# GpSimd takes over the differential pairs' combination in a two-block transformer kernel

## The chip, the cores and the metric

The kernel runs on one core of one Trainium2 chip. Its time is the device time of one execution in microseconds (us), and a kernel's number is the median of several executions. The core has a matrix engine (TensorE, PE in the rows; PEld is its weight load), a vector engine (VectorE, DVE), a scalar engine (ScalarE, ACT), GpSimd (POOL) and SyncE (SP), which starts most transfers. They run side by side and wait for each other by semaphores. Each works off its own list strictly in order.

## What is computed

Two transformer blocks of two layers each run one after the other over 512 tokens of width 1024, in float32 ("three-product" matmuls split each operand in a high and a low part). The change touches only the attention of the second block. It has three kinds of heads:

```python
# second block, hybrid_layer: 6 "a" heads (dilated), 4 "b" heads (differential), 6 "c" heads (causal)
def probs(q, k):                     # one 128-row block of queries
    s = jnp.einsum('bqhd,bkhd->bhqk', sl(q), k).astype(jnp.float32) * scale + bias
    return jax.nn.softmax(jnp.where(causal, s, -jnp.inf), axis=-1)
a = probs(q1, k1) - lam * probs(q2, k2)
return jnp.einsum('bhqk,bkhd->bqhd', a.astype(v.dtype), v)
...
o_b = (rms_norm(o_b, subln_g, SUBLN_EPS) * (1.0 - lam_init)).astype(x.dtype)
...
heads = jnp.concatenate([o_a.reshape(Bn, S, -1), o_b.reshape(Bn, S, -1), o_c.reshape(Bn, S, -1)], axis=-1)
h = layer_norm(DEEPNORM_ALPHA * x + heads @ w_o, ln1_g, ln1_b)
```

A differential head thus needs two score matrices, whose exponentials are combined as first + ratio * second (the ratio has the sign, lambda and both row sums in it) before they meet the values.

## The kernel before

The attention of a layer is a list of 80 units (`UNITS`): one head and one block of 128 queries each, 128, 256, 384 or 512 keys wide (the block's row i gives 128(i+1) keys). A "b" head takes two units that stand next to each other, `first` and `second`; there are 16 such pairs. The first 8 units (`EARLY`, four pairs) are worked off among the projections. The other 12 pairs, whose `second` is unit 9, 13, 18, 23, 28, 33, 38, 42, 47, 52, 57 or 62, are spread among 48 units of "a" and "c" heads. For this loop every engine has its own list by steps. In step s:

- TensorE makes the scores of unit s (`score`, lines 2248, 2249 and 2252) into one of three PSUM banks, then the transposes of unit s-4 (line 2367; a pair only has those of its `second`, which wait for the combination, `s_paired`). Two ranks after a group's last transposes `mix` multiplies the group's transposed probabilities with the values (line 2346). After a head's last group `turn_chunk` transposes a 128-column chunk of the output `ao` (line 2325), in the steps of `turn_at`.
- VectorE adds mask and bias and takes the row minimum or maximum (`scored`, line 2986), from PSUM into one of five SBUF buffers `sc2` ("sc" in the rows). A buffer is taken again five units later, when its unit was transposed, or, for a `first`, when its pair was combined. Then come, if due, `pair(s-2)` (two small operations for the ratio, lines 2994 and 2995, and one SCALAR_TENSOR_TENSOR over the unit, line 2996), `rows_out2` (divides a finished group's rows by their sums into `ao`, lines 3050 to 3062), and `lo_part` (the low part of a transposed chunk, `g_lo`, line 2530). `sub_norm` (lines 3025 to 3033) normalises the "b" heads' output.
- ScalarE takes the exponentials (`exp2`) and copies the transposes out of PSUM. At steps 24 and 26 it also splits a weight tile.
- GpSimd makes the copies of the keys (`two_keys`, lines 944 and 947, four operations for each "a" head), each when the scores of a named unit are there, and low parts of weight tiles (line 927).

So a pair goes TensorE, VectorE, ScalarE, VectorE, TensorE. A semaphore between two engines, or between two dependent operations of one engine, stands at each arrow.

Of the kernel before, what the change touches and what calls it, by code (L numbers as in the profile page):

```python
# [262 lines left out]
def _program(nc, I, out, seen):  # L263
    ctx = ExitStack()
    with ctx:
# [211 lines left out]
        s_pool_piece = Signal(nc, ctx, seen, "pool_piece")  # L477
        s_product = Signal(nc, ctx, seen, "product")
        s_b_recip = Signal(nc, ctx, seen, "b_recip")
        s_rows_part = Signal(nc, ctx, seen, "rows_part")  # L480
# [289 lines left out]
        ended = {what: GROUPS[group_of[r]][-1] for what, r in last_of.items()}  # L770
        out_step = {what: turn_step[r + 3] if r + 3 <= LAST else STEPS for what, r in ended.items()}
        B_DONE = max(out_step["b", h] for h in range(B_HEADS))
# [143 lines left out]
        def _(pool):  # L916
# [14 lines left out]
            def ctx_lo(l, k):  # L931
# [3 lines left out]
                                   ALU.subtract).then_inc(s_lo_c.sem, s_lo_c.nth((l, k)))  # L935

            def two_keys(y, h):

# [52 lines left out]
            for i, what in enumerate(splits):  # L991
# [19 lines left out]
                if what[1:] == ("o", 0, 0):  # L1011
# [8 lines left out]
                    pool.wait_ge(s_mm.sem, s_mm.at((what[0], "vc", XT - 1)))  # L1020
                    pool.memset(vc[:].rearrange("p t (h d) -> p (t h) d", d=VW)[:, :, HD:VW], 1.0).then_inc(s_vc_ones.sem, s_vc_ones.nth(what[0]))
                if what[1:] == ("o", 0, 1):
                    pool.wait_ge(s_tile_lo.sem, s_tile_lo.at(splits[i - 1]))
                    for h in range(A_HEADS):
                        two_keys(what[0], h)
                for p in range(-(-width(what) // PIECE)):
# [667 lines left out]
        def _(pe):  # L1694
# [475 lines left out]
            for l in range(DEPTH):  # L2170
# [181 lines left out]
                for step in range(FROM, STEPS):  # L2352
# [3 lines left out]
                    if r is not None:  # L2356
# [3 lines left out]
                        if UNITS[i]["second"]:  # L2360
                            pe.wait_ge(s_paired.sem, s_paired.at((y, i)))
                        else:
                            pe.wait_ge(s_probs.sem, s_probs.at((y, i)))
# [151 lines left out]
        def _(dve):  # L2515
# [422 lines left out]
            for l in range(DEPTH):  # L2938
# [50 lines left out]
                def pair(i):  # L2989

                    u = UNITS[i]
                    n, ratio = u["n"], small[:, 2, i % 8:i % 8 + 1]
                    dve.wait_ge(s_probs.sem, s_probs.at((y, i)))
                    step(V.reciprocal(ratio, small[:, 1, i % 8:i % 8 + 1]))
                    step(V.tensor_scalar(ratio, ratio, sums[:, u["sum"]:u["sum"] + 1], lam[:, 4:5], ALU.mult, ALU.mult))
                    V.scalar_tensor_tensor(probs_of(i)[:, 0:n], probs_of(i)[:, 0:n], ratio, probs_of(i - 1)[:, 0:n],
                                           ALU.mult, ALU.add).then_inc(s_paired.sem, s_paired.nth((y, i)))
# [68 lines left out]
                for st in range(EARLY, STEPS):  # L3066
                    if st - 2 == EARLY + 1:
                        pair(st - 2)
                    if turns(st) is not None and turns(st) >= 3:
                        rows_out2(turns(st) - 3)  # L3070
                    if st < len(UNITS):
                        u = UNITS[st]
                        if st >= EARLY + N_B and UNITS[st - N_B]["first"]:
                            dve.wait_ge(s_paired.sem, s_paired.at((y, st - N_B + 1)))
                        elif st >= EARLY + N_B:
# [8 lines left out]
                    sub_norm(st)  # L3084
                    if st - 2 in turn_at:
                        k = turn_at[st - 2]
                        dve.wait_ge(s_kr_all.sem, s_kr_all.at((y, C_HEADS - 1)))
                        lo_part(g_lo[:, CHUNKS.index(k), :], ps[:, TURNED["chunk", k], :], g_hi[:, CHUNKS.index(k), :], (y, "m", k), (y, "m", k))
                assert B_DONE + 2 < STEPS
                for r in range(LAST - 2, LAST + 1):  # L3090
                    rows_out2(r)
# [235 lines left out]
```

## Time and profile before

| | us |
|---|---|
| median of 3 runs | 1830.54 (1830.51 to 1833.87) |
| the profiled execution | 1828.74 |
| its span in the profile | 1826.9 |
| attention loop, first layer of the second block | 744.4 to 823.6 |
| attention loop, second layer | 1342.3 to 1421.5 |

Busy over the span: PE 1779.0 us (97%), DVE 1196.8 (66%), ACT 912.8 (50%), POOL 777.8 (43%). TensorE's granted clock is 0.998 of full speed. The profiled execution lasts 1.84 us longer than its span. Times of events are counted from the span's start. Each of the two loops runs from the scores of unit 10 to the end of the last `mix`.

### The profile page before, as it was taken

Reading aid. Unit: us, or ns where it says so; the run is one execution under the profiler, and the core shown is the slowest. Engines: PE = TensorE matmul, PEld = TensorE weight load, DVE = VectorE, ACT = ScalarE, POOL = GpSimd, SP = SyncE. Lnnn points to the kernel's source line nnn. Section 1 sums busy time; section 2 is a strip of 40 time slices with the busy share of each in tenths; the row PEclk is TensorE's granted clock in tenths of the full one; section 3 lists DMA queues with packets and bytes.
Section 4 is the critical chain, followed back from the end, with each engine's and each line's share of the span. In section 5 each row is a group of like instructions: output and inputs, shape, how many; then the busy total and the mean of one; then the engine's idle time right before and its main releaser. Section 6 shows DMA issues by size and latency. Waiting matters only on the chain.

```text
span 1826.9 us, 33474 instructions
## 1 busy us (share of the span) xinstructions
PE 1779.0 (97%) x13078; PEld 1585.0 (87%) x13078; DVE 1196.8 (66%) x2313; ACT 912.8 (50%) x1789; POOL 777.8 (43%) x601
## 2 busy tenths in 40 slices
PE   9999999999999999989999999999998999999997
PEld 7898888878898888678999998888877899999886
DVE  5797465269455353785999984256368589998533
ACT  4242276484366474883545443227488255444323
POOL 2544262255553454344443436544424354343652
PEclk9999999999999999999999999999999999999999
DMA  8444141123221232103232323222310323323321
GB/s 337 168 173 167 24 116 60 69 70 139 104 48 55 88 102 107 42 2 139 93 111 98 116 93 126 100 88 92 117 42 2 138 72 114 116 93 116 116 93 46
DMA packets 37032, 182.40 MB, mean 100 GB/s; under 512 B 8288, under 2 KB 9184, under 8 KB 18956
## 3 DMA queue, kind: packets, MB, share of 16 engines
q1 hardware_dynamic: 30664, 168.89, 26.5%
q10 hardware_dynamic: 6212, 11.36, 2.0%
q8 instruction: 106, 1.74, 0.4%
q14 instruction: 50, 0.41, 0.1%
HBM read 178.10 MB, written 5.41 MB: 100 GB/s over the span
## 4 chain that ended last, share of the span: by engine, by line
PE 85%; DVE 8%; ACT 4%; issue 2%; POOL 1%; DMA 1%; DVEq 0%; SPq 0%; ACTq 0%
PE ps L1718 17%; PE ps L1720 17%; PE ps L1719 17%; PE ps L2441 7%; PE ps L2443 7%; PE ps L2442 7%; PE ps L1798 2%; PE ps L1812 2%; PE ps L2346 2%; PE ps L2252 2%; PE ps L1779 1%; PE ps L2367 1%; DVE sc L2986 1%; POOL w_lo L927 1%; ACT pt L1184 1%
## 5 line engine op out<-in xcount | busy, mean ns | idle before, releaser
L927 POOL TENSOR_TENSOR w_lo<-raw,w_hi 128x512 fp32r<-128x512 f32 (+1 forms) x343 | 477.9, 1426 | 616.1 <-ACT w_hi L1057 615.9
L1057 ACT ACTIVATE w_hi<-raw 128x1024 fp32r<-128x1024 f32 (+3 forms) x174 | 170.9, 1026 | 225.8 <-PE ps L1720 208.8
L1033 POOL TENSOR_TENSOR w_lo<-raw,w_hi 128x512 fp32r<-128x512 f32 x80 | 112.7, 1408 | 222.9 <-ACT w_hi L1122 222.7
L1718 PE MATMUL ps<-h_hi,w_lo 128*128 128x512 f32 (+1 forms) x496 | 177.2, 357 | 3.7 <-DVE h_lo L2530 3.6
L1719 PE MATMUL ps<-h_lo,w_hi 128*128 128x512 f32 (+1 forms) x496 | 174.5, 352 | 0.0
L1720 PE MATMUL ps<-h_hi,w_hi 128*128 128x512 f32 (+1 forms) x496 | 174.5, 352 | 0.0
L1718 PE MATMUL ps<-w_hi,hid_lo 128*128 128x512 f32 x352 | 137.1, 390 | 0.0
L1719 PE MATMUL ps<-w_lo,hid_hi 128*128 128x512 f32 x352 | 137.0, 389 | 0.0
L1720 PE MATMUL ps<-w_hi,hid_hi 128*128 128x512 f32 x352 | 136.9, 389 | 0.0
L2530 DVE TENSOR_TENSOR hid_lo<-hid,hid_hi 128x512 fp32r<-128x512 f32 x44 | 65.4, 1529 | 102.1 <-ACT hid_hi L1158 102.1
L1718 PE MATMUL ps<-w_hi,g_lo 128*128 128x512 f32 (+3 forms) x320 | 114.1, 356 | 1.5 <-POOL w_lo L927 1.5
L1720 PE MATMUL ps<-w_hi,g_hi 128*128 128x512 f32 (+3 forms) x320 | 112.1, 350 | 0.0
L1719 PE MATMUL ps<-w_lo,g_hi 128*128 128x512 f32 (+3 forms) x320 | 111.8, 349 | 0.0
L1718 PEld LDWEIGHTS ps<-h_hi,w_lo 128*128 128x128 f32 x496 | 93.8, 189 | 18.6 <-issue 5.5
L1720 PEld LDWEIGHTS ps<-h_hi,w_hi 128*128 128x128 f32 x496 | 93.7, 189 | 12.9
L1719 PEld LDWEIGHTS ps<-h_lo,w_hi 128*128 128x128 f32 x496 | 93.8, 189 | 11.7
L2592 DVE SCALAR_TENSOR_TENSOR acc<-raw,cond,acc 128x512 f32<-128x512 f32 x112 | 98.9, 953 | 0.8 <-DMA raw<-in_tiles 0.7
L1122 ACT ACTIVATE ext_hi<-ps 128x512 fp32r<-128x512 f32 x80 | 47.8, 598 | 95.1 <-DVE ps L3163 69.6
L2441 PE MATMUL ps<-T_hi,w_lo 128*128 128x256 f32 x320 | 90.7, 283 | 0.0
L2441 PE MATMUL ps<-G_hi,w_lo 128*128 128x256 f32 x320 | 90.6, 283 | 0.0
L2442 PE MATMUL ps<-G_lo,w_hi 128*128 128x256 f32 x320 | 90.6, 283 | 0.0
L2443 PE MATMUL ps<-G_hi,w_hi 128*128 128x256 f32 x320 | 90.6, 283 | 0.0
(392 smaller groups left out, 5446.0 us busy)
## 6 DMA issues: line engine op xcount, KB each, us to landing
raw<-in_tiles SPq DMA_DIRECT2D x139, 1024.0 KB, 4.8
strips<-bias_rows ACTq DMA_DIRECT2D x18, 256.0 KB, 4.0
raw<-in_tiles SPq DMA_DIRECT2D x4, 832.0 KB, 4.2
bias_rows<-bias_row SPq DMA_DIRECT2D x10, 320.0 KB, 9.9
raw<-in_tiles SPq DMA_DIRECT2D x4, 768.0 KB, 5.1
res<-in_x SPq DMA_DIRECT2D x2, 1024.0 KB, 6.4
ln<-in_ln_g ACTq DMA_DIRECT2D x4, 512.0 KB, 5.0
ln<-in_ln_b ACTq DMA_DIRECT2D x4, 512.0 KB, 7.6
```

The costliest lines, as they stand in the source:

```text
L927: pool.tensor_tensor(w_lo[:, i % SPLIT, a:e], raw_of(what)[:, a:e], w_hi[:, i % SPLIT, a:e].bitcast(F32), ALU.subtract).then_inc(s_tile_lo ...
L1033: pool.tensor_tensor(lo, quad_of(what[0], j, name), hi.bitcast(F32), ALU.subtract).then_inc(s_pool_piece.sem, s_pool_piece.nth(((what[0], ...
L1057: act.activation(w_hi[:, i % SPLIT, a:b], raw_of(what)[:, a:b], ACT.Copy).then_inc(s_tile_hi.sem, s_tile_hi.nth((what, n)))
L1122: act.activation(piece_of(y, j, name)[0], src, ACT.Copy).then_inc(s_piece_hi.sem, s_piece_hi.nth((what, name)))
L1718: pe.matmul(o, lhs[1], rhs[0], start=first, stop=False)
L1719: pe.matmul(o, lhs[0], rhs[1], start=False, stop=False)
L1720: return pe.matmul(o, lhs[0], rhs[0], start=False, stop=last)
L2441: pe.matmul(o, lhs[1], rhs[0], start=starts and k == 0, stop=False, skip_group_check=True)
L2442: pe.matmul(o, lhs[0], rhs[1], start=False, stop=False, skip_group_check=True)
L2443: m = pe.matmul(o, lhs[0], rhs[0], start=False, stop=ends and k == 3, skip_group_check=True)
L2530: V.tensor_tensor(dst, src, hi.bitcast(F32), ALU.subtract).then_inc(s_lo.sem, s_lo.nth(key))
L2592: V.scalar_tensor_tensor(to[:], w, by, to[:], ALU.mult, ALU.add).then_inc(s_weigh.sem, s_weigh.nth((what, k, h)))
```

## The change

VectorE still computes the ratio of the 12 late pairs. The SCALAR_TENSOR_TENSOR over the unit leaves its list and becomes two operations of GpSimd: a multiplication by the ratio in place (TENSOR_SCALAR), a wait for itself, and the addition of the first's probabilities (TENSOR_TENSOR). TensorE, and VectorE before it reuses the first's buffer, wait for GpSimd. GpSimd's copies of the keys are put among these pairs. Besides, `rows_out2` comes one rank later in VectorE's list, the chunks' transposes (`turn_at`) and `sub_norm` one step later as a result, and `lo_part` one more step behind the transposes. The four early pairs stay as they were.

```diff
-        out_step = {what: turn_step[r + 3] if r + 3 <= LAST else STEPS for what, r in ended.items()}
+        out_step = {what: turn_step[r + 4] if r + 4 <= LAST else STEPS for what, r in ended.items()}
...
+            SECONDS = [x for x in range(EARLY, len(UNITS)) if UNITS[x]["second"]]
+            SOON_PAIRS = [x for x in SECONDS if x < 26]
+            LATE_PAIRS = [x for x in SECONDS if x >= 26]
+
+            def keys_behind(h):
+
+                scored = SCORED_LAST["c", 3 + h] if h < 3 else SCORED_LAST["a", h - 3]
+                return max(x for x in LATE_PAIRS if x <= max(scored, LATE_PAIRS[0]))
+
+            def pool_pair(y, x):
+
+                n = UNITS[x]["n"]
+                pool.wait_ge(s_ratio.sem, s_ratio.at((y, x)))
+                p_ = probs_of(x)[:, 0:n]
+                pool.tensor_scalar(p_, p_, small[:, 2, x % 8:x % 8 + 1], None, ALU.mult).then_inc(s_weighted.sem, s_weighted.nth((y, x)))
+                pool.wait_ge(s_weighted.sem, s_weighted.at((y, x)))
+                pool.tensor_tensor(p_, p_, probs_of(x - 1)[:, 0:n], ALU.add).then_inc(s_pool_paired.sem, s_pool_paired.nth((y, x)))
+                pool.wait_ge(s_pool_paired.sem, s_pool_paired.at((y, x)))
...
+                    for x in SOON_PAIRS:
+                        pool_pair(what[0], x)
                 if what[1:] == ("o", 0, 1):
                     pool.wait_ge(s_tile_lo.sem, s_tile_lo.at(splits[i - 1]))
-                    for h in range(A_HEADS):
-                        two_keys(what[0], h)
+                    for x in LATE_PAIRS:
+                        pool_pair(what[0], x)
+                        for h in range(A_HEADS):
+                            if keys_behind(h) == x:
+                                two_keys(what[0], h)
...
-                            pe.wait_ge(s_paired.sem, s_paired.at((y, i)))
+                            if i > EARLY:
+                                pe.wait_ge(s_pool_paired.sem, s_pool_paired.at((y, i)))
+                            else:
+                                pe.wait_ge(s_paired.sem, s_paired.at((y, i)))
...
-                    step(V.tensor_scalar(ratio, ratio, sums[:, u["sum"]:u["sum"] + 1], lam[:, 4:5], ALU.mult, ALU.mult))
+                    m = V.tensor_scalar(ratio, ratio, sums[:, u["sum"]:u["sum"] + 1], lam[:, 4:5], ALU.mult, ALU.mult)
+                    if i > EARLY:
+                        m.then_inc(s_ratio.sem, s_ratio.nth((y, i)))
+                    else:
+                        step(m)
+                    if i > EARLY:
+                        return
                     V.scalar_tensor_tensor(probs_of(i)[:, 0:n], probs_of(i)[:, 0:n], ratio, probs_of(i - 1)[:, 0:n],
                                            ALU.mult, ALU.add).then_inc(s_paired.sem, s_paired.nth((y, i)))
...
-                    if turns(st) is not None and turns(st) >= 3:
-                        rows_out2(turns(st) - 3)
+                    if turns(st) is not None and turns(st) >= 4:
+                        rows_out2(turns(st) - 4)
...
-                            dve.wait_ge(s_paired.sem, s_paired.at((y, st - N_B + 1)))
+                            dve.wait_ge(s_pool_paired.sem, s_pool_paired.at((y, st - N_B + 1)))
...
-                    if st - 2 in turn_at:
-                        k = turn_at[st - 2]
+                    if st - 3 in turn_at:
+                        k = turn_at[st - 3]
                         dve.wait_ge(s_kr_all.sem, s_kr_all.at((y, C_HEADS - 1)))
                         lo_part(g_lo[:, CHUNKS.index(k), :], ps[:, TURNED["chunk", k], :], g_hi[:, CHUNKS.index(k), :], (y, "m", k), (y, "m", k))
+                for k in [turn_at[s] for s in sorted(turn_at) if s + 3 >= STEPS]:
+                    lo_part(g_lo[:, CHUNKS.index(k), :], ps[:, TURNED["chunk", k], :], g_hi[:, CHUNKS.index(k), :], (y, "m", k), (y, "m", k))
...
-                for r in range(LAST - 2, LAST + 1):
+                for r in range(LAST - 3, LAST + 1):
```

GpSimd's list in the first layer's loop, before, from the keys of the third "a" head to those of the fourth (free_hi and free_lo hold a head's keys in high and low part):

```order
L944 CAST free_hi_155<-ka 64x512 [waits scores,k_low]
L944 CAST free_hi_155<-ka 64x512 [waits k_twice]
L947 TENSOR_TENSOR free_lo_158<-ka,free_hi_155 64x512 [waits k_twice]
L947 TENSOR_TENSOR free_lo_158<-ka,free_hi_155 64x512 [waits k_low]
L944 CAST free_hi_153<-ka 64x512 [waits scores,k_low]
L944 CAST free_hi_153<-ka 64x512 [waits k_twice]
L947 TENSOR_TENSOR free_lo_156<-ka,free_hi_153 64x512 [waits k_twice]
L947 TENSOR_TENSOR free_lo_156<-ka,free_hi_153 64x512 [waits k_low]
```

The same stretch of the changed kernel:

```order
L966 CAST free_hi_155<-ka 64x512 [waits scores,pool_paired]
L966 CAST free_hi_155<-ka 64x512 [waits k_twice]
L969 TENSOR_TENSOR free_lo_158<-ka,free_hi_155 64x512 [waits k_twice]
L969 TENSOR_TENSOR free_lo_158<-ka,free_hi_155 64x512 [waits k_low]
L954 TENSOR_SCALAR sc_4_149<-sc_4_149,small 128x128 [waits ratio,k_low]
L956 TENSOR_TENSOR sc_4_149<-sc_4_149,sc_3_148 128x128 [waits weighted]
L966 CAST free_hi_153<-ka 64x512 [waits scores,pool_paired]
L966 CAST free_hi_153<-ka 64x512 [waits k_twice]
L969 TENSOR_TENSOR free_lo_156<-ka,free_hi_153 64x512 [waits k_twice]
L969 TENSOR_TENSOR free_lo_156<-ka,free_hi_153 64x512 [waits k_low]
L954 TENSOR_SCALAR sc_4_149<-sc_4_149,small 128x384 [waits ratio,k_low]
L956 TENSOR_TENSOR sc_4_149<-sc_4_149,sc_3_148 128x384 [waits weighted]
```

The pairs of units 52 (128 wide) and 57 (384 wide) now stand behind four key operations each, which wait for scores of their own.

VectorE's list before, from the finished rows of a group ahead of unit 63 to the combination of pair 62 (ISA is `scored`, with a second row for its row result):

```order
L3053 RECIPROCAL recips<-sums 128x1
L3056 RECIPROCAL recips<-ps 128x4 [waits mixed]
L3057 TENSOR_TENSOR ao<-ps,recips 128x4x64 [waits dve_step]
L3062 TENSOR_SCALAR ao<-ps,recips 128x64 [waits b_recip]
L2986 ISA sc_0_145,small<-ps,strips 128x256 [waits scores,strips,turned]
L2986 ISA small 128x1
L2986 ISA sc_1_146,small<-ps,strips 128x512 [waits scores,strips,turned]
L2986 ISA small 128x1
L2994 RECIPROCAL small<-small 128x1 [waits probs]
L2995 TENSOR_SCALAR small<-small,sums,lam 128x1 [waits dve_step]
L2996 SCALAR_TENSOR_TENSOR sc_4_149<-sc_4_149,small,sc_3_148 128x256 [waits dve_step]
```

The same place of the changed kernel:

```order
L3016 ISA sc_0_145,small<-ps,strips 128x256 [waits scores,strips,turned]
L3016 ISA small 128x1
L2560 TENSOR_TENSOR g_lo<-ps,g_hi 128x512 [waits hi,kr_all]
L3089 RECIPROCAL recips<-sums 128x1
L3092 RECIPROCAL recips<-ps 128x4 [waits mixed]
L3093 TENSOR_TENSOR ao<-ps,recips 128x4x64 [waits dve_step]
L3098 TENSOR_SCALAR ao<-ps,recips 128x64 [waits b_recip]
L3016 ISA sc_1_146,small<-ps,strips 128x512 [waits scores,strips,turned]
L3016 ISA small 128x1
L3024 RECIPROCAL small<-small 128x1 [waits probs]
L3025 TENSOR_SCALAR small<-small,sums,lam 128x1 [waits dve_step]
```

Unit 63's `scored` has moved ahead of the group's rows, a chunk's low part (which stood before unit 62) has come in between, and both now stand between `scored` of unit 63 and `scored` of unit 64, which the ratio follows. The combination itself is gone.

## Rows read from the trace of the kernel before

**Rows 1.** Busy time by stage, the attention loop of each layer; (x) counts instructions.

```profile
core 0: us, PE busy (x) PEld busy (x) DVE busy (x) ACT busy (x) POOL busy (x), PEclk, DMA share, GB/s
744.40:823.60 79.20, 69.98 (x942) 56.72 (x942) 60.65 (x236) 65.82 (x171) 30.84 (x34) 1.00 0.08 22
1342.30:1421.50 79.20, 69.97 (x942) 56.73 (x942) 60.63 (x236) 65.80 (x171) 30.82 (x34) 1.00 0.08 22
```

**Rows 2.** Waits of PE in the first layer's loop: total us, times, longest.

```profile
PE ps L2367 <- DVE sc L2996: 6.8, 8, 1.5
PE ps L2346 <- DVE g_lo L2530: 0.8, 1, 0.8
PE ps L2252 <- DVE small L2986: 0.8, 1, 0.8
```

**Rows 3.** DVE groups by form, same loop: busy us, mean ns, idle before.

```profile
L3057 DVE TENSOR_TENSOR ao<-ps,recips 128x256 f32<-128x256 f32 x12 | 5.1, 425 | 1.0 <-PE ps L2346 0.6
...
L2530 DVE TENSOR_TENSOR g_lo<-ps,g_hi 128x512 fp32r<-128x512 f32 x5 | 3.5, 692 | 3.6 <-ACT g_hi L1616 3.6
...
L2996 DVE SCALAR_TENSOR_TENSOR sc<-sc,small,sc 128x512 f32<-128x512 f32 x3 | 3.1, 1036 | 0.1
...
L2996 DVE SCALAR_TENSOR_TENSOR sc<-sc,small,sc 128x256 f32<-128x256 f32 x3 | 2.4, 795 | 0.1
...
L2996 DVE SCALAR_TENSOR_TENSOR sc<-sc,small,sc 128x128 f32<-128x128 f32 x3 | 2.0, 661 | 0.1
...
L3056 DVE RECIPROCAL recips<-ps 128x4 f32<-128x4 f32 x11 | 1.9, 174 | 4.3 <-PE ps L2346 4.2
L2996 DVE SCALAR_TENSOR_TENSOR sc<-sc,small,sc 128x384 f32<-128x384 f32 x3 | 1.9, 619 | 0.1
```

**Rows 4.** The chain that ended last, 766.5 to 770 us; start us, us, what.

```profile
766.72 0.69 DVE sc L2986
...
767.84 0.76 DVE sc L2996
...
768.65 0.66 PE ps L2367 x4
```

**Rows 5.** POOL groups by form, whole span.

```profile
L947 POOL TENSOR_TENSOR free_lo<-ka,free_hi 64x512 fp32r<-64x512 f32 x24 | 31.5, 1314 | 1.9
L944 POOL CAST free_hi<-ka 64x512 fp32r<-64x512 f32 x24 | 14.6, 610 | 34.6 <-PE ps L2252 21.0 <-PE ps L2249 12.8
...
L969 POOL CAST q_parts<-q 64x768 fp32r<-64x768 f32 x6 | 4.9, 822 | 16.1 <-PE ps L1779 16.0
...
L927 POOL TENSOR_TENSOR w_lo<-raw,w_hi 128x128 fp32r<-128x128 f32 x4 | 2.9, 718 | 0.0
...
L927 POOL TENSOR_TENSOR w_lo<-raw,w_hi 128x16 fp32r<-128x16 f32 x1 | 0.2, 224 | 0.0
```

**Rows 6.** POOL in order of time; brackets hold idle before and releaser.

```profile
787.68 2.96 POOL L947 TENSOR_TENSOR free_lo<-ka,free_hi 64x512 fp32r<-64x512 f32 x2
792.87 1.28 POOL L944 CAST free_hi<-ka 64x512 fp32r<-64x512 f32 x2 [2.23 <-PE ps L2249]
794.24 2.65 POOL L947 TENSOR_TENSOR free_lo<-ka,free_hi 64x512 fp32r<-64x512 f32 x2
```

**Rows 7.** DVE in order of time, around two of the combinations.

```profile
787.90 1.61 DVE L2996 SCALAR_TENSOR_TENSOR sc<-sc,small,sc 128x512 f32<-128x512 f32 x1
...
797.33 0.62 DVE L2996 SCALAR_TENSOR_TENSOR sc<-sc,small,sc 128x384 f32<-128x384 f32 x1
```

**Rows 8.** PE in order of time: the first transposes of one combined unit.

```profile
798.01 0.55 PE L2367 MATMUL ps<-ident,sc 128*128 128x128 f32 x3 [0.66 <-DVE sc L2996]
```

**Rows 9.** DVE in order of time, the end of the loop.

```profile
809.72 1.22 DVE L3025 TENSOR_TENSOR sq_b<-ao 128x1024 f32<-128x1024 f32 x1
...
814.31 0.69 DVE L2530 TENSOR_TENSOR g_lo<-ps,g_hi 128x512 fp32r<-128x512 f32 x1
```

**Rows 10.** PE in order of time, the end of the loop.

```profile
815.05 1.39 PE L2346 MATMUL ps<-va,raw 128*64 128x65 f32 x40
```

More of the change, by code:

```diff
@@ L478, in _program @@
         s_product = Signal(nc, ctx, seen, "product")
+        s_ratio = Signal(nc, ctx, seen, "ratio")
+        s_pool_paired = Signal(nc, ctx, seen, "pool_paired")
+        s_weighted = Signal(nc, ctx, seen, "weighted")
         s_b_recip = Signal(nc, ctx, seen, "b_recip")
```

## The prediction

> **What bounds the kernel now.** The table of busy time comes first: TensorE is busy for 97% of the span, so a change elsewhere can only act where TensorE is not. I then cut the two attention loops of the second block out, the only stretches in which the changed lists differ. In each, 79.2 us long, TensorE is busy for 70.0 us, ScalarE 65.8, VectorE 60.6 and GpSimd 30.8 [rows 1]. The two layers agree to 0.02 us, so I work one out and double it. TensorE idles 9.2 us per layer; the list of who waited for whom says for what: 6.8 us, in 8 of the 12 late pairs, for the combined probabilities of line 2996; 0.8 for a low part, and 0.8 for a score bank that VectorE had not emptied [rows 2]. So all 12 combinations are on the path or near it, and eight have no slack at all.
>
> The next question is what is late in such a wait: VectorE's throughput or the length of the way round. At pair 28, the chain goes from TensorE's scores through `scored` (766.72, 0.69 us), the ratio, the combination (767.84 to 768.60) to the transposes at 768.65 [rows 4]. VectorE had idled before, and nothing but the length of the way counts. VectorE is itself the late one at two of the eight, pairs 47 and 62: there the combination is stretched, 1.61 us at 787.90 for a form whose mean is 1.04 and includes this one [rows 3, 7], and the longest wait of TensorE, 1.5 us, is for pair 62 [rows 2].
>
> **The change, part by part (per layer).**
>
> *The combination itself.* VectorE's twelve cost 3.1 + 1.9 + 2.4 + 2.0 = 9.4 us as measured, stretched ones included [rows 3]; with a start 0.02 us behind the ratio [rows 4] 9.6. GpSimd's first operation, a multiplication in place, is not in the trace. The nearest rows are casts, also with one input: 0.61 us for 512 columns, 0.82 for 768 [rows 5], so 0.19 + 0.00083 per column. Nothing in the trace says that a one-input operation can be faster than that cast, so it is the lower bound; the upper one is its two-input operation, 1.31 us for 512. I take the cast: 0.61, 0.50, 0.40, 0.29 us for 512, 384, 256, 128 columns. The second is the two-input form: 1.31 us for 512, 0.22 for 16 [rows 5], so by a straight line 1.02, 0.75, 0.47 for the others (the 128-column row says 0.72, which is my upper bound for that width). A start behind another operation takes 0.09 us (794.15 to 794.24) [rows 6]; there are two. That makes 2.10, 1.71, 1.33 and 0.94 us, three times each: 18.2 us. The way round gets 18.2 - 9.6 = 8.6 us longer over twelve pairs. Four pairs, two of 384 and two of 128 columns, are not waited for now; on the path they would be worth 2 x (1.71 - 0.64) + 2 x (0.94 - 0.68) = 2.7 us, and I count half. **Term a: 8.6 - 1.3 = 7.3 us.**
>
> *The shared list of GpSimd.* Four key operations take 4.0 us (792.87 to 796.89) [rows 6], and a pair behind them waits for all four. They were free to run late, since their "a" heads come steps later. Now the ratio of pair 47 is there at 787.90 [rows 7]: GpSimd is done with it at 790.0, with the third keys at 794.0, with pair 52 at 794.9, with the fourth keys at 798.9. The ratio of pair 57 is ready at 797.3 [rows 7], and TensorE stands waiting for that pair now (0.66 us at 798.01) [rows 8]. It starts 1.6 us late, less the 0.4 by which pair 47's own longer product moves both. **Term b: 1.2 us.** The keys themselves stay hidden.
>
> *VectorE's list.* Behind `scored` of unit 63 now stand a low part (0.69 us) and a group's rows (0.17 + 0.42 and two small ones, about 0.8 in sequence) [rows 3], then `scored` of unit 64 and the ratio of pair 62. Before, the low part was two places earlier and the rows ahead of unit 63. At worst 1.2 us of this comes out at TensorE, and 0.35 and 0.4 at pairs 23 and 28, where rows now stand in front of the last `scored` ahead of a ratio. Against it VectorE loses waits: 4.2 us for `mix` ahead of the rows and 3.6 for ScalarE ahead of the low parts [rows 3]. These helped nobody by being there, but most of them lie where the next `scored` waits for TensorE's scores anyway, so their end gives little. I take half. **Term c: 1.0 us.**
>
> *The end of the loop.* The chunk of step 73 (before 72) has its low part in step 76 (before 74). It frees the PSUM bank of the `mix` that TensorE has in step 77. Now it ends at 815.00 and `mix` starts at 815.05 [rows 9, 10]: no slack. In between come two more `scored` and a group's rows (0.4 + 0.7 + 0.6 us), of which VectorE has some in hand since it need not wait for `mix`. **Term d: 1.0 us.**
>
> *What costs nothing:* the new semaphores on TensorE (a wait replaces a wait), and VectorE's wait for GpSimd before it reuses a `first`'s buffer. Behind it are queued the `scored` four and five units after the pair's second. TensorE needs their banks only after the pair's own transposes, so its wait covers this one; without that cover it would cost up to the 1.3 us by which a 512-column product is longer. The early pairs, and all work outside the loops, do not change; no transfer moves.
>
> *A rule on the memory ports.* VectorE's combination took 1.61 us at 787.90 while GpSimd ran two-input operations from 787.68, which themselves took 2.96 us against 2.65 for the same two at 794.24 [rows 6, 7]; at 767.84, with GpSimd idle, 0.76 was enough [rows 4]. My sum contains this stretch as a gain, since it goes by the measured 9.4 us and leaves VectorE with almost nothing of this kind. What is left is the squaring at 809.72, 1.22 us, with two inputs from SBUF [rows 9]: the last keys, which move behind pair 62, could now run beside it. The Trainium skill (SBUF — State Buffer, "SBUF: two separate sides") says that GpSimd and a VectorE operation with two SBUF inputs take the shared port pair as an exclusive lock, held for the whole instruction. By that rule the squaring would wait for up to one GpSimd operation, 1.3 us by the row of such a one, and term d would be 2.2 instead of 1.0, the time 2.4 us longer in all. The rows of the combination bear the lock out; that the squaring meets it is open, and I leave it out.
>
> *Sum:* 7.3 + 1.2 + 1.0 + 1.0 = 10.5 us per layer, 21 in both. The profiled execution has 1828.7 us (its span, 1826.9, and 1.8 around it), so 1849.7. The median of the runs shown is 1.8 us above that execution: **1851.5 us.**
>
> **The rivals.**
>
> *Faster: VectorE's relief decides.* It loses 9.4 us of operations and up to 7.8 us of waits per layer [rows 3]. If VectorE were what is late at most pairs, the ratio would come earlier by as much as the product is longer. Pairs 47 and 62 speak for it, and the 0.8 us for a score bank [rows 2]; pair 28 and the idle before it speak against. It decides where the ratio comes more than 1.3 us earlier. With all 8.4 us of the three waits gone the time would be 1814; with the half of it that those places could give, 4 us per layer, 1822. Chance 0.11.
>
> *No change.* The relief and the longer way cancel: 1827 to 1834. Chance 0.07. That the move is not made is excluded: the lists show it.
>
> *Partly absorbed.* Lateness at one pair is taken up by slack before the next, as after unit 62, and the list terms vanish; half of term a or somewhat more stays: 3 to 7 us per layer, 1837 to 1844. For it speaks that TensorE does not wait at four pairs. Chance 0.24.
>
> *More costly.* If GpSimd's multiplication costs as much as its two-input operation, each product is 0.7, 0.5, 0.35 or 0.2 us longer, 5.2 us per layer, so 1862; with the squaring's 2.4 it is 1864. Chance 0.10.
>
> **How the numbers follow.** The forecast (8 to 14 us per layer: 1846 to 1859) has 0.48. Slower by more than 0.2%, about what a measurement of this kernel can tell from no change (3.7 us), are the forecast, the partly absorbed and the more costly case, 0.82; the same 0.07; faster 0.11. The range leaves out the faster case and the lowest of "no change", and above only what is beyond the sum of both upper bounds: 1832 to 1866. Slower cases alone would be 1837 to 1864.
>
> **What would show it.** In the changed profile each loop is about 10 us longer, with TensorE's busy time still near 70 us. TensorE's largest wait at the transposes is for GpSimd's addition, some 12 to 17 us per layer, in nine or more pairs. GpSimd's operations on "sc" number 24 per layer and sum to about 16 us; the multiplication of 512 columns takes about 0.6 us (above 1 would be the costly case). The longest wait is at pair 57, behind key copies. VectorE's busy time in the loop falls by about 9 us, and its waits for `mix` ahead of the rows nearly vanish. The last `mix` but two waits for a low part. I would be wrong if the ratios came much earlier after the pair's scores than now, in other words if the stretch from `scored` of a second's follower to its ratio shrank by over 1 us at most pairs, or if GpSimd's operations were much shorter than the rows of its casts.

## The result, and the profile after

The changed kernel takes 1888.2 us (median of 4, 1884.3 to 1891.6) against 1830.5 (1829.6 to 1833.9): ratio 1.031, 95% interval 1.029 to 1.033. It is slower by 57.7 us, where 21 were forecast, and lies outside the range of 1832 to 1866. The profiled execution has a span of 1882.5 us.

The two loops, cut so that each holds the same 942 matmul records as in [rows 1]:

```profile
core 0: us, PE busy (x) PEld busy (x) DVE busy (x) ACT busy (x) POOL busy (x), PEclk, DMA share, GB/s
745.40:851.60 106.20, 78.66 (x942) 62.79 (x942) 52.33 (x224) 66.92 (x171) 53.62 (x58) 0.90 0.06 16
1370.20:1477.00 106.80, 78.25 (x942) 63.20 (x942) 53.09 (x224) 66.89 (x171) 53.66 (x58) 0.92 0.06 16
```

They take 106.2 and 106.8 us instead of 79.2, together 54.6 of the 55.6 us by which the span grew. The last 1.0 us lies ahead of the loops; executions of the kernel before alone differ by more. TensorE's idle time rose from 9.2 to 27.5 us in the first, and its busy time from 70.0 to 78.7, for the same work: the granted clock, 1.00 before, is 0.90. VectorE is busy 8.3 us less, GpSimd 22.8 more.

What TensorE and VectorE wait for in the first layer's loop (us, times, longest):

```profile
PE ps L2397 <- POOL sc L956: 24.5, 11, 4.0
PE ps L2373 <- DVE g_lo L2560: 2.4, 2, 1.5
```

```profile
DVE sc L3016 <- POOL sc L956: 20.2, 10, 2.9
...
DVE recips L3092 <- PE ps L2373: 1.2, 1, 1.2
```

Where [rows 2] had 6.8 us in eight places for VectorE's combination, there are 24.5 in eleven for GpSimd's addition. The second list shows a wait that the prediction put at no cost: VectorE, now behind GpSimd for a `first`'s buffer, stands for 20.2 us (whether that costs time is taken up below). Its wait for `mix` ahead of the rows went from 4.2 us [rows 3] to 1.2, as forecast.

GpSimd's groups by form (busy us, mean ns), 3 of each kind per layer:

```profile
L954 POOL TENSOR_SCALAR sc<-sc,small 128x512 f32<-128x512 f32 x3 | 4.7, 1567 | 3.2 <-DVE small L3025 3.2
L956 POOL TENSOR_TENSOR sc<-sc,sc 128x512 f32<-128x512 f32 x3 | 3.8, 1263 | 0.3
L954 POOL TENSOR_SCALAR sc<-sc,small 128x384 f32<-128x384 f32 x3 | 3.7, 1245 | 4.5 <-DVE small L3025 4.4
...
L956 POOL TENSOR_TENSOR sc<-sc,sc 128x384 f32<-128x384 f32 x3 | 3.0, 992 | 0.2
L954 POOL TENSOR_SCALAR sc<-sc,small 128x256 f32<-128x256 f32 x3 | 2.8, 924 | 14.6 <-DVE small L3025 14.6
L956 POOL TENSOR_TENSOR sc<-sc,sc 128x256 f32<-128x256 f32 x3 | 2.2, 723 | 0.2
L954 POOL TENSOR_SCALAR sc<-sc,small 128x128 f32<-128x128 f32 x3 | 1.8, 605 | 12.9 <-DVE small L3025 12.8
L956 POOL TENSOR_TENSOR sc<-sc,sc 128x128 f32<-128x128 f32 x3 | 1.4, 454 | 0.2
```

The addition came out as worked out from [rows 5] (1.26, 0.99, 0.72, 0.45 us against 1.31, 1.02, 0.75, 0.47). The multiplication costs 1.57, 1.25, 0.92 and 0.61 us, where 0.61, 0.50, 0.40 and 0.29 were put and 1.31 for 512 columns was the upper bound. With the two starts of 0.09, twelve products make 25.5 us, not 18.2, against VectorE's 9.6.

Some of TensorE's waits in order of time (start us, us; in brackets the idle time before), and below them its granted clock by stretches of 5 us (the value ahead of the last two):

```profile
751.80 1.11 PE L2397 MATMUL ps<-ident,sc 128*128 128x128 f32 x4 [3.55 <-POOL sc L956]
...
771.05 0.44 PE L2397 MATMUL ps<-ident,sc 128*128 128x128 f32 x2 [2.00 <-POOL sc L956]
```

```profile
779.95 0.66 PE L2397 MATMUL ps<-ident,sc 128*128 128x128 f32 x4 [3.95 <-POOL sc L956]
```

```profile
750.00:755.00 5.00, 3.20 (x22) 2.12 (x24) 0.87 (x4) 0.33 (x2) 1.67 (x2) 0.50 0.02 3
755.00:760.00 5.00, 3.79 (x41) 2.75 (x38) 1.97 (x9) 3.02 (x8) 1.06 (x2) 0.83 0.25 63
765.00:770.00 5.00, 3.46 (x17) 2.10 (x17) 3.52 (x18) 3.48 (x9) 1.27 (x2) 1.00 0.03 8
775.00:780.00 5.00, 1.05 (x8) 0.69 (x6) 2.02 (x13) 2.26 (x7) 3.89 (x3) 1.00 0.00 0
780.00:785.00 5.00, 5.00 (x37) 3.95 (x39) 1.40 (x7) 3.13 (x9) 0.00 (x0) 0.66 0.01 3
```

After the wait of 3.55 us the clock of the stretch is 0.50 (1.2 instead of 2.4 GHz all the time), after that of 3.95 it is 0.66, while from 760 to 780, with waits of 1.21, 0.79 and 2.00 us, it is 1.00. A lower clock also follows the waits of 2.60, 3.42 and 3.01 us at pairs 42, 57 and 62. The profile before has no wait above 1.51 us in the loops and no such stretch. The four transposes at 751.80 take 1.11 us; four at 779.95, just before the clock falls, 0.66.

The first loop reads as if long waits made the clock fall and short ones did not. The second does not bear that out. There the clock falls behind the wait of 2.00 us at pair 23, and stays at 1.00 behind one of 3.47 us at pair 62:

```profile
1395.26 0.69 PE L2397 MATMUL ps<-ident,sc 128*128 128x128 f32 x2 [2.00 <-POOL sc L956]
...
1454.91 0.44 PE L2397 MATMUL ps<-ident,sc 128*128 128x128 f32 x2 [3.47 <-POOL sc L956]
```

```profile
1395.00:1400.00 5.00, 4.74 (x63) 4.13 (x64) 1.40 (x4) 2.79 (x6) 4.92 (x5) 0.66 0.01 2
...
1455.00:1460.00 5.00, 5.00 (x85) 4.70 (x85) 2.23 (x9) 3.46 (x9) 4.65 (x6) 1.00 0.01 3
```

### The profile page after: what moved, and what is told of

Same layout as the page of the kernel before. It is cut to its first block, busy times and chain, and to the rows that moved or that the text cites. A ratio compares the mean times of both kernels' runs of the same rounds, so it can differ in the third digit from the quotient of the medians.

```text
span 1882.5 us, 33520 instructions
## 1 busy us (share of the span) xinstructions
PE 1796.8 (95%) x13078; PEld 1598.5 (85%) x13078; DVE 1181.1 (63%) x2289; ACT 914.6 (49%) x1789; POOL 822.9 (44%) x649
## 4 chain that ended last, share of the span: by engine, by line
PE 83%; DVE 7%; POOL 4%; ACT 4%; issue 2%; DMA 1%; DVEq 0%; SPq 0%; POOLq 0%; ACTq 0%
PE ps L1745 17%; PE ps L1747 16%; PE ps L1746 16%; PE ps L2471 7%; PE ps L2473 7%; PE ps L2472 7%; PE ps L1825 2%; PE ps L1839 2%; PE ps L2397 2%; PE ps L2373 2%; PE ps L1806 1%; POOL sc L954 1%; PE ps L2279 1%; POOL sc L956 1%; ACT w_hi L1084 1%
## 5 line engine op out<-in xcount | busy, mean ns | idle before, releaser
L2397 PE MATMUL ps<-ident,sc 128*128 128x128 f32 x300 | 59.6, 304 | 49.5 <-POOL sc L956 49.5
L1747 PEld LDWEIGHTS ps<-h_hi,w_hi 128*128 128x128 f32 x496 | 93.7, 189 | 12.9
L2397 PEld LDWEIGHTS ps<-ident,sc 128*128 128x128 f32 x300 | 39.6, 154 | 66.1 <-POOL sc L956 54.8
```

The lines of the kernel that those rows point to most:

```text
L1747: return pe.matmul(o, lhs[0], rhs[0], start=False, stop=last)
L2397: m = pe.transpose(ps[:, b, P * j:P * j + P], probs_of(i)[:, P * j:P * j + P], ident[:])
```

## The experiments

Times are medians, and ratios are to runs of the kernel before made together with each kernel (its medians: 1830.0 to 1831.3 us). Excesses over it are against these.

**The list change alone.** The kernel before, VectorE combines:

```diff
-        out_step = {what: turn_step[r + 3] ...
+        out_step = {what: turn_step[r + 4] ...
...
-                        rows_out2(turns(st) - 3)
+                        rows_out2(turns(st) - 4)
...
-                    if st - 2 in turn_at:
+                    if st - 3 in turn_at:
...
```

> The kernel before with only the second half of the change: rows_out2 one rank later, the chunks' transposes one step later, lo_part three steps behind them; VectorE still combines. Theory A (GpSimd's longer product on TensorE's way round is the loss, the clock falls in its wake): this part alone costs little, 1827 to 1837 us (my terms c and d were 2 us per layer, of which VectorE's saved waits may give some back), TensorE's granted clock stays at full speed. Theory L (the later rows and low parts are what TensorE waits for): a third or more of the loss, 1848 us or more.

1844.2 us, ratio 1.006 (1.005 to 1.008), 12.9 us slower: between the two theories, and three times terms c and d. Of the 15.5 us by which its span is longer, 3.6 lie ahead of the loops, where nothing was changed; each loop is 5.9 us longer. TensorE's clock does fall (0.98 in both loops), which theory A had excluded.

**GpSimd's part alone,** the changed kernel with those lines set back:

> The changed kernel with the list part undone: GpSimd combines the twelve pairs, rows_out2, turn_at and lo_part stand as before. Theory A: nearly the whole loss stays, 1880 to 1895 us. Theory L: 1870 us or less.

1881.3 us, ratio 1.027 (1.026 to 1.029), as theory A said. GpSimd's part is 50 of the 57.7 us, and the lists add only 6.9 on top of it, where alone they cost 12.9: some of their lateness may hide behind the longer products (no run shows where).

**A cheaper multiplication.** First a copy in place (it leaves the ratio out of the result), then a multiplication in another form, each in place of the same line (arguments are left out at "..."):

```diff
-                pool.tensor_scalar(p_, p_, small[...], None, ALU.mult)...
+                pool.tensor_copy(p_, p_)...
```

```diff
-                pool.tensor_scalar(p_, p_, small[...], None, ALU.mult)...
+                pool.tensor_tensor(p_, p_, small[...].broadcast_to((P, n)), ALU.mult)...
```

> The changed kernel with GpSimd's multiplication by the ratio replaced by a plain copy in place (the ratio is left out of the result). The copy's rows of before say 0.61 us for 512 columns against 1.57 measured for the multiplication; over the twelve pairs the product gets shorter by 3 x (0.96 + 0.75 + 0.52 + 0.32) = 7.7 us per layer. Theory A: TensorE's waits fall by about that, 15 us in all, and most of the slow-clock stretches (9 us of longer matmuls per layer) go with the long waits: 1858 to 1874 us. Theory L or a loss by the mere number of hand-overs: the waits hardly depend on the product's length, 1883 us or more.

> The changed kernel, with GpSimd's multiplication written as a two-input operation that reads the ratio as a column repeated over the width; the result is the same. Theory L (the length of the product is what TensorE waits for, at all twelve pairs): the addition, also of two inputs, took 1.26, 0.99, 0.72 and 0.45 us for 512, 384, 256 and 128 columns, the multiplication 1.57, 1.25, 0.92 and 0.61, so each product is 0.31, 0.25, 0.20 or 0.15 us shorter, three times each: 2.7 us per layer, 5.5 us in all, and up to 2 more where TensorE's clock then does not fall: 1881 to 1884. Theory H (what counts is the number of hand-overs and the place in GpSimd's list, not the length): 1887 to 1889. A third case, that the repeated column is read as slowly as before: no change in the rows of line 954, 1887 to 1889.

The copy: 1870.1 us, ratio 1.021 (1.020 to 1.023). The two-input form: 1880.0 (1871.9 to 1881.8), ratio 1.027 (1.025 to 1.028); its profiled execution is the fastest one. In their profiles, first the copy's, then the other's:

```profile
L954 POOL COPY sc<-sc 128x512 f32<-128x512 f32 x3 | 1.8, 610 | 1.8 <-DVE small L3025 1.5 <-POOL free_lo L969 0.3
```

```profile
L954 POOL TENSOR_TENSOR sc<-sc,small 128x512 f32<-128x512 f32 x3 | 3.1, 1040 | 3.4 <-DVE small L3025 3.1 <-POOL free_lo L969 0.3
```

The copy costs what the prediction gave the multiplication (0.61 us). The multiplication of two inputs, the second a repeated column, costs 1.04 us, less than the addition and two thirds of the one-input form. Theory L's 1881 to 1884 rested on 1.26 us for it; it was shorter, 8.8 us in all instead of 5.5, and 8.2 us came back, with executions 10 us apart. All four lie below theory H's range, so theory L holds. The copy's time lies in theory A's range, but half of the reason given failed: the slow-clock stretches did not go with the shorter products. The clock is 0.91 and 0.90 in its loops, and TensorE is busy as long as in the changed kernel (table below).

**The addition alone** (the ratio is left out of the result):

> The changed kernel without GpSimd's multiplication: only the addition stands (this leaves the ratio out of the result). A product is then 1.26, 0.99, 0.72 or 0.45 us long, 11.4 us per layer with starts, where the copy in place made 17.9, the two-input multiplication 21.2 and the changed kernel 25.6. Theory L (time goes by the summed length of the products, with the clock's fall in it; the copy gave 18.1 us for 15.3 us of length, 1.18 per us): 13.0 us less length than with the copy, 13 to 15.4 us less time, 1855 to 1857. Theory F (a floor: other waits, the ratio's own way or the moved rows, take over): 1860 or more.

1851.3 us, ratio 1.011 (1.009 to 1.013), less than either theory said. The loops in the profiled executions (columns as in [rows 1]), of the addition alone, of the copy, and of the list change alone from above:

```profile
747.05:837.25 90.20, 75.23 (x942) 59.74 (x942) 52.20 (x224) 66.18 (x171) 40.68 (x46) 0.94 0.07 19
1355.90:1444.70 88.80, 73.82 (x943) 58.80 (x942) 52.22 (x224) 66.23 (x172) 40.71 (x46) 0.96 0.07 20
```

```profile
746.70:844.70 98.00, 77.92 (x941) 63.04 (x942) 52.10 (x224) 66.77 (x171) 46.05 (x58) 0.91 0.07 18
1363.30:1463.00 99.70, 79.21 (x943) 64.02 (x942) 52.33 (x225) 66.79 (x172) 46.15 (x58) 0.90 0.06 18
```

```profile
747.95:833.10 85.15, 72.40 (x942) 58.05 (x942) 58.85 (x236) 66.53 (x171) 30.86 (x34) 0.98 0.07 20
1353.10:1438.20 85.10, 72.05 (x942) 57.98 (x941) 58.91 (x236) 66.22 (x170) 29.88 (x33) 0.98 0.08 21
```

Side by side, with the length of twelve products per layer and TensorE's idle and busy time over both loops in the profiled execution (us; of the two-input form that is the fastest, 1871.9):

| kernel | length | median time | both loops | TensorE idle | TensorE busy |
|---|---|---|---|---|---|
| before | 9.6 | 1830.5 | 158.4 | 18.5 | 140.0 |
| list change alone | 9.6 | 1844.2 | 170.3 | 25.8 | 144.5 |
| addition alone | 11.4 | 1851.3 | 179.0 | 30.0 | 149.0 |
| copy | 17.9 | 1870.1 | 197.7 | 40.6 | 157.1 |
| two inputs | 21.1 | 1880.0 | 200.5 | 46.8 | 153.7 |
| changed | 25.5 | 1888.2 | 213.0 | 56.1 | 156.9 |

From the addition alone to the changed kernel the length grows by 28.2 us over both layers and the median time by 36.9, 1.3 for 1. The rows say where this comes from: TensorE's idle time grows by 26.1 us, nearly 1 for 1, so little of the length is absorbed; its busy time, for the same matmuls, grows by 7.9. (The 2.9 us missing to 36.9 are the medians' distance from the profiled executions.) With only 1.8 us more length per layer than VectorE's, the shortest still costs 21 us. In its loops it has 11.5 us more idle time than the kernel before, which 3.6 us of length and the 7.3 of the list change nearly make up, and 9.0 more busy time.

**TensorE kept at work.** The changed kernel; TensorE transposes the identity into the free bank before it waits:

```diff
+                        if UNITS[i]["second"] and i > EARLY:
+                            pe.wait_ge(*emptied[b])
+                            for j in range(4 * (UNITS[i]["n"] // P)):
+                                pe.transpose(ps[:, b, P * (j % 4):P * (j % 4) + P], ident[:], ident[:])
```

> The changed kernel with idle time filled: ahead of its wait for each of the twelve pairs TensorE transposes the identity 4, 8, 12 or 16 times (for 128 to 512 columns, about 0.11 us each) into the bank that the pair's transposes overwrite. The results are the same. If the slow clock after the long waits costs by itself (theory A: 9 us per layer beside 18 of waiting), the granted clock stays near full speed and the time falls by 8 to 18 us, 1870 to 1880. If the slow clock only fills time in which TensorE would have waited anyway, nothing is won and the filling costs where the wait is shorter than it: 1888 or more.

1877.2 us, ratio 1.025 (1.023 to 1.026): work that nobody needs made the kernel 11.0 us faster by the medians, and 6.5 by the spans of the profiled executions (1876.0 and 1882.5). Its loops:

```profile
core 0: us, PE busy (x) PEld busy (x) DVE busy (x) ACT busy (x) POOL busy (x), PEclk, DMA share, GB/s
746.80:846.70 99.90, 83.91 (x1061) 69.53 (x1061) 53.06 (x224) 66.12 (x171) 53.66 (x58) 1.00 0.06 18
1365.40:1470.60 105.20, 89.72 (x1062) 74.86 (x1062) 52.42 (x224) 66.69 (x171) 53.60 (x58) 0.94 0.06 17
```

In the first the clock is 1.00 and the loop 6.3 us shorter than the changed kernel's; in the second it still fell somewhere (0.94), and the loop is 1.6 us shorter. TensorE's waits for the addition are the same in both, to 0.01 us each; what differs is the clock and with it the busy time, 5.8 us more in the second. So the clock's part is shown. As the fall was not wholly prevented, and the transposes at some pairs end after the addition that they fill the wait for (by 1.0 and 1.6 us in all in the two loops), 7 to 11 us is a lower bound.

**All three together.** Lists set back, the two-input multiplication, and the filler:

> GpSimd combines as in the changed kernel, but with the list change undone, the multiplication in its shorter two-input form, and TensorE transposing the identity into the free bank (4 to 16 times) ahead of its wait for each late pair. Each of the three alone made the changed kernel faster: 6.9, 8.2 and 11.0 us. Theory S (three separate terms that add): 1888.2 - 26.1 = 1862, and the granted clock is 1.00 in the loops. Theory O (they overlap: with shorter waits the clock falls less anyway, so the filler has less to give): 1865 to 1872. What is above 1830 in it is then the longer product alone.

1856.6 us, ratio 1.014 (1.013 to 1.016), 5 us under the sum and below both theories. The clock is 0.98 and 1.00 in its loops, the waits for the addition are 6.7 us in the first. What stays, 26 us, goes with 2 x (21.1 - 9.6) = 23 us of longer products. But up to 4 of them may be the filler's own: at pairs 18, 33 and 38 its transposes end 1.17, 0.60 and up to 0.26 us after GpSimd's addition.

**The queue in GpSimd's list.** In the changed kernel the first four of the six groups of key copies stand one pair later:

```diff
-                scored = SCORED_LAST["c", 3 + h] if h < 3 else SCORED_LAST["a", h - 3]
-                return max(x for x in LATE_PAIRS if x <= max(scored, LATE_PAIRS[0]))
+                return (38, 47, 52, 57, 62, 62)[h]
```

> The changed kernel, with each group of key copies one pair later in GpSimd's list (behind pairs 38, 47, 52, 57, 62, 62). Theory Q (term b of the prediction: pairs 57 and 52 stand behind key copies): the product of pair 57 started 0.9 us after its ratio, that of pair 52 1.1 us after it; both would start within 0.1 us of the ratio, and the time falls by 1.8 us (57 alone) to 4 us (both): 1884 to 1887. Theory K (the copies have no slack left, TensorE's scores of a later head wait for them): 1889 to 1895, with TensorE waiting for GpSimd's casts or low parts of keys. No effect: 1888.

1891.1 us, ratio 1.034 (1.032 to 1.035), 2.9 slower by the medians, with executions that overlap (1890.4 to 1892.3, and 1884.3 to 1891.6). The chain of the changed kernel shows the queue itself, copies and then pair 57 (start us, us):

```profile
814.93 1.30 POOL free_lo L969
816.30 1.28 POOL free_lo L969
...
817.66 1.25 POOL sc L954
818.99 1.00 POOL sc L956
820.04 0.55 PE ps L2397 x3
```

The ratio was ready at 816.77; the product starts at 817.66, 0.9 us later. But the experiment did not take the queue away: in it pair 57 still starts 0.87 us behind its ratio, pair 42 got copies in front too (wait 3.12 us, before 2.60), and the clock is 0.50 from 830 to 835 us and 0.66 from 845 to 850, where it was 0.82 and 1.00. What moved is only that a group now stands in front of pair 42; the ones in front of 52 and 57 were replaced by their neighbours. So the run says nothing of what term b is worth.

**The two list pieces apart.** The kernel before with the rows alone one rank later, then with the low part alone one step later:

> The kernel before with one piece of the list change alone: a group's rows are written one rank later (4 ranks behind its turn, not 3); low parts where they were, VectorE combines. The prediction's term c, without the low part: about 0.8 us per layer, 1832 to 1834. The theory from the trace with both list pieces (there the wait for pair 62 grew from 1.51 to 2.96 us and TensorE's clock fell behind it, about 1.4 us): the rows alone put 0.8 us in front of pair 62's ratio and 1.0 us on the earlier pairs, the wait stays near 2.3 us and the clock does not fall: 1.5 to 2 us per layer, 1834 to 1836.

> The kernel before with the other piece alone: each low part one step later (3 steps behind its turn, not 2); rows where they were, VectorE combines. The prediction's term d and the low part of term c: 1.0 + 0.6 us per layer, 1834 to 1835. The theory from the trace with both pieces: at the end of the loop TensorE's mix came 1.9 us later, and 0.7 us at pair 62, no fall of the clock: 2.6 us per layer, 1836 to 1838. In both theories the sum of this kernel's excess and that of the rows alone is less than the 12.8 us that both pieces cost together if the fall of the clock needs both at once; if the pieces simply add, it is 12 to 13.

The rows: 1840.6 us, ratio 1.005 (1.004 to 1.007), 10.6 slower. The low part: 1830.0, ratio 1.000 (0.999 to 1.001), no change. Both expectations erred, in opposite directions. The two layers of the rows' profile, by the same 942 matmuls:

```profile
core 0: us, PE busy (x) PEld busy (x) DVE busy (x) ACT busy (x) POOL busy (x), PEclk, DMA share, GB/s
746.70:832.20 85.50, 72.50 (x942) 58.25 (x943) 60.51 (x237) 66.66 (x171) 30.84 (x34) 0.98 0.07 20
1350.80:1433.30 82.50, 70.73 (x942) 56.60 (x942) 58.47 (x236) 66.43 (x171) 31.07 (x34) 1.00 0.08 21
```

79.2 became 85.5 in one and 82.5 in the other. They part at pair 62. VectorE's combination in the first layer, and TensorE's waits there and near the end of the loop:

```profile
807.72 1.58 DVE L2996 SCALAR_TENSOR_TENSOR sc<-sc,small,sc 128x256 f32<-128x256 f32 x1
```

```profile
809.35 0.44 PE L2367 MATMUL ps<-ident,sc 128*128 128x128 f32 x2 [2.79 <-DVE sc L2996]
...
823.47 1.39 PE L2346 MATMUL ps<-va,raw 128*64 128x65 f32 x40 [1.31 <-DVE g_lo L2530]
```

In the second layer the combination takes 0.57 us and the wait is 1.62. In the first it meets a two-input operation of GpSimd's key copies and takes 1.58, the wait is 2.79 (1.51 before), and the clock of the following 5 us is 0.66. The wait of 1.31 us for a low part, new in both, stands at the last `mix` but one. It comes from the rows: with `out_step` TensorE's transposes of that chunk move a rank back too, and `g_hi` and `g_lo` with them.

**No meeting on the ports.** On the kernel before, GpSimd holds its two-input operations for keys 0, 1, 2 and 4 until a pair is combined; then the same with the rows moved:

```diff
+                if h in (0, 1, 2, 4):
+                    pool.wait_ge(s_paired.sem, s_paired.at((y, {0: 33, 1: 42, 2: 47, 4: 62}[h])))
```

> The kernel before, with the two-input operations of GpSimd's key copies for heads 0, 1, 2 and 4 held until VectorE has combined pair 33, 42, 47 or 62; nothing else changes. In the trace of before those four combinations were stretched from 0.35, 0.49, 0.75 and 0.49 us to 1.22, 0.79, 1.61 and 1.10 because they met such an operation, and TensorE waited for three of them (0.91, 0.69, 1.51 us). Theory P (the meeting itself costs the path): 0.3 + 0.7 + 0.6 us per layer come back, 3.2 in all, 1826 to 1829, and all twelve combinations have their short times. Theory N (the slack behind takes it, or the keys are late in turn): 1830 to 1833.

> Rows one rank later, as in the kernel with the rows alone (1840.6 us), and GpSimd's two-input operations of the key copies held behind pairs 33, 42, 47 and 62, as in the kernel after that name (1828.9). In the kernel with the rows alone the combination of pair 62 took 1.58 us (1.10 before) because it was later and so met more of a key operation; TensorE's wait for it grew from 1.51 to 2.79 us and its granted clock then fell to 0.66 for 5 us. Theory M (the 10 us of the rows are 0.8 us in front of pair 62 plus what that lateness meets: the key operation and the clock): without the meeting the wait is 1.7 to 1.9 us, the clock stays, 1.1 + 1.5 us per layer come back, 1834 to 1836. Theory R (the moved rows cost it by themselves, at many pairs): only the 1.5 us of the held keys come back, 1838 to 1840.

On the kernel before: 1828.9 us, ratio 0.999 (0.998 to 1.000), the only version ahead of both kernels, by about 1.5 us, at the edge of what can be told. Its combinations, to be read beside [rows 3], and TensorE's waits:

```profile
L2998 DVE SCALAR_TENSOR_TENSOR sc<-sc,small,sc 128x512 f32<-128x512 f32 x3 | 2.3, 752 | 0.1
...
L2998 DVE SCALAR_TENSOR_TENSOR sc<-sc,small,sc 128x384 f32<-128x384 f32 x3 | 1.9, 619 | 0.1
...
L2998 DVE SCALAR_TENSOR_TENSOR sc<-sc,small,sc 128x256 f32<-128x256 f32 x3 | 1.5, 484 | 0.1
...
L2998 DVE SCALAR_TENSOR_TENSOR sc<-sc,small,sc 128x128 f32<-128x128 f32 x3 | 1.1, 369 | 0.1
```

```profile
PE ps L2369 <- DVE sc L2998: 5.2, 7, 1.3
PE ps L2250 <- DVE small L2988: 1.4, 2, 0.8
```

The stretch is gone in all forms (1036 to 752 ns, 795 to 484, 661 to 369), TensorE waits 1.6 us less per layer for pairs, but 1.4 us in two places for a score bank that VectorE had not emptied (line 2250 is 2248 of the kernel before, which has 0.4 us in one place); the loop is 0.4 us shorter. With the rows moved: 1838.4 us, ratio 1.004 (1.003 to 1.006). The wait at pair 62 is 1.70 and 1.52 us and the clock does not fall behind it; but only 2.1 us came back. Of the two theories R fits: the rows themselves cost about 3 us per layer (82.15 us for the first loop), and the meeting and the fall of the clock behind it, where they happen, another 3 (85.5 against 82.5).

## Why the prediction was wrong

*What bounds the loops* was read rightly: TensorE's waits for pairs, the ratio's way round and not VectorE's throughput. The faster rival fell for the reason given against it. The forecast was that ten or so us per layer come; 27 came.

*Term a failed by the price of one operation.* The lengthening is 25.5 - 9.6 = 15.9 us per layer, not 8.6. The step that failed is "the nearest rows are casts, also with one input". Only the number of inputs was compared, not the arithmetic; and "the upper one is its two-input operation" was no bound. The discount for four pairs "not waited for now" was wrong too: eleven pairs of twelve wait, and TensorE's idle time in the length series grows nearly as much as the length. The costly rival had the right mechanism with 0.10, and was itself too low, 1864, as it stopped at 1.31 us. The Trainium skill (GPSIMD Engine Reference, "Engine selection") has one-input operations on GpSimd as "roughly line-rate": the copy agrees (0.61 us for 512 columns), the multiplication at 1.57 does not.

*A step was missing: TensorE's clock.* "TensorE's busy time still near 70 us" was taken as given; it is 78.7 and 78.3. Rows of before could not show it, since the clock is 1.00 throughout both loops; but the prediction itself forecast longer waits and never asked what TensorE does after them. At least 7 to 11 of the 57.7 us are this. (The longest wait is not at pair 57 behind key copies, 3.42 us, as forecast, but at pair 28, 3.95; with the lists set back that wait is 3.34.) The Trainium skill (TensorE: Matmul & The Clock Gate, "What's actually happening") says that TensorE's clock is set by how busy it has been; the rows agree in that filling its idle time raised the clock (0.90 to 1.00 in the first loop). A prediction that lengthens waits has to price it.

*Terms c and d* were 2.0 us per layer; the lists cost 6.5 alone and 3.5 with the rest. The place at pair 62 and the end of the loop were right. The cause of d was not: the low part's own step costs nothing (its waits for ScalarE fall from 3.6 to 1.3 us); the end of the loop is late because moving the rows moves the chunk's transposes. And the rows delay TensorE at five of the late pairs, not at three, by 0.1 to 0.6 us each in the second loop of the rows' profile (the wait at pair 28 is 1.66 us instead of 1.05, at pair 42 1.34 instead of 0.91).

*Term b* is right as a row (0.9 us of queue at pair 57, forecast 1.2), and its effect on the time was not isolated.

*The wait "covered" by TensorE's own.* VectorE stands 20.2 us for GpSimd, but the prediction's reason for putting this at nothing holds as far as the trace shows: in the chain of work that ended last GpSimd's addition is followed by TensorE, nine times in each loop of the changed kernel, and never by VectorE. A run with a sixth buffer, without the wait, was not made.

*The squaring.* It took 1.22 us again, with GpSimd idle: the last key operation ended at 837.06 and the squaring began at 837.42. So the lock that the prediction weighed for it did not meet it, by 0.4 us. It met the combinations instead, in the kernel before as in the one with moved rows.

*Where the 57.7 us are,* from single undoings: 6.9 the lists, 11.0 the filler, 8.8 us the avoidable length of the multiplication (8.2 measured). Together undone they gave 31.6, 5.5 more than the sum, and of the 26 us left 23 are the longer products that GpSimd has even so. The rows split the loops' 54.6 us another way: 37.6 are idle time of TensorE, of which the added length is 31.8 and the list change alone had 7.3; 17.0 are its longer busy time. The second number is not the clock's price, since slower matmuls also fill time in which TensorE would have waited. No sharper split is claimed.

## What to carry over

Price an operation on another engine by a row of the same operation there, and where there is none, let the upper bound go well beyond the nearest row; a two-input form can be the cheaper one. When a change lengthens TensorE's waits, put the clock into the range: the same matmuls may then take longer, and cheap matmuls ahead of the wait can win time. When a list entry is moved, follow what hangs on its step in the other engines' lists before pricing the entry itself.

## What the runs showed of the hardware

- GpSimd, 128 partitions, float32, 512 columns: copy 0.61 us, multiplication by a column read as repeated second input 1.04, addition of two tiles 1.26, multiplication by a per-partition scalar operand 1.57. Per column, from 128 to 512: 0.8, 1.7, 2.1 and 2.5 ns.
- TensorE's clock fell from 2.4 to 1.2 GHz inside loops in which TensorE is busy for 74% of the time (the changed kernel), but the length of a single wait does not say when: a fall followed 2.00 us and none followed 3.47 in the same loop; with the rows moved and the keys held it fell (0.84 and 0.82 from 1350 to 1360 us) behind a wait of 1.32. The filler's kernel has the same waits in both its loops, and 1.00 in one and 0.94 in the other, 5.3 us apart.
- VectorE's combination is stretched by up to 1.1 us (0.48 to 1.58 for 256 columns) where it meets GpSimd's two-input operations on keys, and by none where those are held.
